# Who issues the down weights of the experts: ScalarE, behind its copy of the product, in place of SyncE

## The reference

```
u = x*(1+scale) + shift                       # (320, 1024)
s = sigmoid(u @ w_router)                     # 64 experts in 8 groups
idx, w = the best 8 experts of the best 4 groups, weights scaled to sum 2.5
routed = sum over the 8: w * ((silu(u @ w_gate[e]) * (u @ w_up[e])) @ w_down[e])
y = routed + swiglu(u, shared weights)
x = LayerNorm(alpha*x + (1+gate)*y)
```

## Time and profile before

| | |
|---|---|
| median of three runs | 2154.64 us |
| time of the profiled execution | 2159.98 us |
| its span, first to last instruction | 2158.5 us |
| TensorE busy in matmuls | 1803.2 us (84%) |
| VectorE, ScalarE, GpSimd busy | 705.2, 305.6, 364.2 us |
| experts of layer 0, first product to last | 397.1 to 951.4 us |
| experts of layer 1, first product to last | 1557.2 to 2098.9 us |

### The profile page before, as it was taken

The page is one execution under the profiler, slowest core; times in us unless marked ns, Lnnn a source line. Parts: engine busy times, 40 slices in busy tenths (PEclk is TensorE's granted clock), DMA queues, the critical chain, the costliest instruction groups (busy, mean ns, idle before and its releaser), DMA issues. The chain is left out here.

```text
span 2158.5 us, 32756 instructions
## 1 busy us (share of the span) xinstructions
PE 1803.2 (84%) x12297; PEld 1043.4 (48%) x12298; DVE 705.2 (33%) x1785; ACT 305.6 (14%) x639; POOL 364.2 (17%) x469
## 2 busy tenths in 40 slices
PE   6998977688888987775999998988488889987775
PEld 4555644344445543442556555544344455544442
DVE  1111237312233332216302444443611423331226
ACT  0221211000111110100122222221110111110010
POOL 3000100222222222210001012110022222222210
PEclk8999988799999999988798799997699999999997
DMA  9488965699999999959324389981699999999976
GB/s 348 147 314 307 366 231 234 259 424 416 387 383 403 418 411 393 408 229 333 105 70 162 103 275 284 294 279 66 270 402 422 415 399 404 422 408 407 403 290 219
DMA packets 133127, 675.12 MB, mean 313 GB/s; under 512 B 28432, under 2 KB 41360, under 8 KB 92709
## 3 DMA queue, kind: packets, MB, share of 16 engines
q1 hardware_dynamic: 84880, 570.20, 66.9%
q10 hardware_dynamic: 22180, 56.23, 7.7%
q0 software_dynamic: 25968, 47.32, 6.1%
HBM read 651.29 MB, written 47.99 MB: 324 GB/s over the span
## 5 line engine op out<-in xcount | busy, mean ns | idle before, releaser
L2292 PE MATMUL bank<-ring,work 128*64 128x256 f32 x4096 | 536.7, 421 | 143.3 <-DMA ring<-in_exp_w 140.0
L2292 PEld LDWEIGHTS bank<-ring,work 128*64 128x64 f32 x4096 | 340.5, 152 | 308.8 <-issue 130.2
L2020 PE MATMUL bank<-ring,uT 128*128 128x512 f32 (+1 forms) x896 | 256.7, 503 | 1.9 <-ACT work L1002 0.9
L2304 PE MATMUL bank<-ring,work 128*64 128x512 f32 x1032 | 249.9, 605 | 1.3 <-DVE work L1741 1.0
L788 POOL DMA_INDIRECT work<-u_d,work x128 | 130.6, 1020 | 640.5 <-DVE work L1707 334.8
L1707 DVE COPY work<-work 128x1 int32<-128x1 int32 (+1 forms) x128 | 19.3, 153 | 530.5 <-ACT work L1161 529.7
L2020 PEld LDWEIGHTS bank<-ring,uT 128*128 128x128 f32 (+1 forms) x896 | 119.4, 169 | 131.3 <-issue 115.7
L795 POOL DMA_INDIRECT pair_d<-work x128 | 132.6, 1036 | 267.6 <-DVE work L1711 250.1
L1161 ACT ACTIVATE work<-bank 128x128 f32<-128x128 f32 x128 | 35.5, 277 | 674.1 <-PE bank L2292 674.1
L1157 ACT COPY work<-bank 128x512 f32<-128x512 f32 x128 | 74.9, 585 | 292.7 <-PE bank L2304 292.7
L2284 PE MATMUL bank<-ident,work 128*128 128x128 f32 x516 | 97.5, 312 | 21.6 <-DMA work<-u_d,work 21.6
(11 more groups left out here) (357 smaller groups left out, 1721.6 us busy)
## 6 DMA issues: line engine op xcount, KB each, us to landing
ring<-in_exp_w SPq DMA_DIRECT2D x128, 2048.0 KB, 17.9
ring<-in_exp_w SPq DMA_DIRECT2D x128, 1024.0 KB, 13.0
ring<-in_ada_w SPq DMA_DIRECT2D x24, 2048.0 KB, 10.9
ring<-in_cache_k SPq DMA_DIRECT2D x128, 256.0 KB, 4.2
ring<-in_cache_v SPq DMA_DIRECT2D x128, 256.0 KB, 5.5
ring<-in_gla_w_in SPq DMA_DIRECT2D x6, 2048.0 KB, 17.2
ring<-in_kv_w_mod SPq DMA_DIRECT2D x4, 2048.0 KB, 11.4
work<-pair_d ACTq DMA_DIRECT2D x4, 2048.0 KB, 9.6
```

Source lines behind the costliest of these rows:

```text
L2020: ins = mm(out, uT[:, c, t0:t0 + r], ring_pair(unit)[:, c, cols], start=(c == 0), stop=(c == KT - 1), skip_group_check=(t == ST))
L2292: ins = mm(psum[s][64 * c:64 * c + 64, 0:2 * P].rearrange("p (a n) -> p a n", a=2), xT[:, s, j * P + 64 * half:j * P + 64 * half + 64], gu ...
L2304: ins = mm(psum[3 + s][64 * c:64 * c + 64, :], hT[:, s, 64 * f:64 * f + 64], w[:, f, c * 512:(c + 1) * 512], start=(f == 0), stop=(f == 1) ...
```

## The change

SyncE no longer waits for `y_full` and no longer issues the down weights for e from 3 on. ScalarE issues them instead, right behind the copy of the down product of e-1: the transfer of the down weights of e+2, which goes to the same slot. The down weights of the first three experts of each layer are still issued by SyncE.

```diff
                 def steady(e, s):
                     sp.wait_ge(h_full, e + (base - 2))
                     load_expert(l, e, s)
-                    sp.wait_ge(y_full, e + (base - 2))
-                    load_down(l, e, s)
...
+                def load_down(e, s):
+
+                    act.dma_start(ring[:, 3 * s + 2, :],
+                                  W["exp_w"][l, ds(e, 1)].rearrange("o p n -> p (o n)")[:, 2 * UNIT:3 * UNIT])\
+                       .then_inc(unit_full[3 * s + 2], 16)
+
-                def one(e, s, i, first=False):
+                def one(e, s, i, first=False, more=True):
                     act.wait_ge(h_full, e + (base + 1))
                     act.activation(sil[:, s, :], psum[s][:, 0:P], ACT.Silu).then_inc(sem("sil_ready"), 1)
                     if not first:
                         y_out(e - 1, (s + 2) % 3, stored_before(e - 1, (s + 2) % 3, i))
+                        if more:
+                            load_down(e + 2, (s + 2) % 3)
...
                 for e in range(60, 64):
-                    one(e, e % 3, 0)
+                    one(e, e % 3, 0, more=e + 2 < NE)
```

## The result

The changed kernel is slower by a third of a per cent: ratio 1.0035 to the kernel before, 95% interval 1.002 to 1.005 (20 runs of each; medians 2159.68 and 2153.42 us). On the median of the prediction that is 2154.64 x 1.0035 = 2162.2 us, +7.5 us. The forecast was 2154.3 us and no change that can be told; 0.22 was given to slower. The second rival, with half its stalls, had 2162 us too; what follows shows that its mechanism is at most a part of the loss, so that agreement is luck.

A forecast was written before the change was run, and what follows sets the result against it. The expert stages were taken as bound by DMA bytes, not by when transfers are issued. Terms -2.3 + 0 + 2.0 = -0.3 us gave 2154.3 us on the median, range 2145 to 2164.

The forecast's parts named there:

- The second rival: Expert stages, slower: down weights in q10 wait behind load_gate's rows; 2168 us, or 2162 with half the stalls; chance 0.18.
- A third busy queue: Gathers in q0 beside busy q10: they take 9.4 us, issued 13 us ahead at the least; 0, bounds 0 and +2.
- The signs that were named: Expert stages: earlier L620 issue, start hole gone, gate/up landing 20 us or more, down 8 to 10, in_exp_w wait near 140.
- Start of each layer's experts: At 410 to 412 and layer 1's start, earlier gate and up weights fill idle DMA engines: -2.3 us, bounds 0 and -2.8.
- Holes in the middle: Six 20 us stretches around the shared expert lack 9.8 us of DMA share; counted as 0, bounds 0 and -9.8.
- The argument from the lagging engines: In the middle holes the share bottoms at 0.27 and 0.25: engines finishing a transfer never pause, so earlier issue gains 0.
- the holes are real: Faster rival: each of the six middle holes is recovered too, -12.1 us, 2142.5 us, or 2147 with half; chance 0.27.
- Order of the bytes: Down weights share engines with gate and up weights, which land later at the layers' ends: +2.0 us, bounds 0 and +3.9.
- ScalarE's part: One DMA issue per expert on ScalarE, 0.33 to 0.45 us, hidden before a Silu that waits for TensorE: 0.
- Two streams at once: Expert stages: alternating between two queues costs no DMA rate; 0, bounds -3 and +3.
- Down weights behind the row loads: Slower rival: row loads in q10 delay down weights, TensorE waits 4 us at three places; 12 us if engines dry; chance 0.18.
- The rule that was cited: Issuing engines' queues end on the same 16 DMA engines, so the change can move order, not rate; no size.

The follow-up runs named there:

- late issue: Changed kernel with SyncE's old wait put back, gate and up weights of e issued only behind the down product of e-4: 1.0027 of the kernel before.
- the run with short gathers: Changed kernel with layer 1's gathers and scatters cut from 128 to 64 partitions: 0.9965; the kernel before with the same cut 0.9957, so 1.0008 between them.
- the run with rows of 8 KB: Changed kernel with gate and up weights in two transfers of 128 rows of 8 KB: 1.0031 of the kernel before.
- the one with even and odd halves: Changed kernel with gate and up weights in two transfers, of the 64 even and the 64 odd partitions: 1.0005 of the kernel before.
- the one-queue kernel: Kernel before with gate and up weights issued early and down weights after them, both by SyncE in q1: 0.9972 of the kernel before.

## Why the prediction was wrong

- **The step that failed** is "A third busy queue", put at 0 with bounds of 0 and +2 us. It took the 9.4 us of rows 10, where q10 carried rows of 4 KB for a while, as what gathers take beside a second queue. The gathers went to 15.9 us, TensorE's wait for them from 21.6 to 155.4 us, and with the second queue of weights the time is 0.27% (late issue) to 0.63% (early issue) longer than without it. The working for the rivals had the tool at hand, in "on an engine q10 must pass 8 + 28 + 8 rows, each beside one of 16 KB": turns by row. It was never applied to q0, whose gather and scatter have 8 rows each per expert and engine, in 8 packets and 2 small ones. Before, these 10 met 18 packets in one other queue; after, they meet 9 and 9 in two queues, and every queue gets one turn in a round. What is shown is that the second queue of weights costs the time. That it does so through the gathers is argued: for it are the waits and the run with short gathers; against it as the whole cause are the run with rows of 8 KB (no such waits, 1.0031), the one with even and odd halves (128.8 us of them, 1.0005), and the stage of layer 1 that shrank with the stall as well. How the loss divides between the gathers, the down weights behind the row loads and the clock that fell behind a long wait (0.66 from 1985 to 2005) stays open.
- **The signs that were named**: issue to landing was to rise for gate and up weights to 20 us or more, and to fall for down weights to some 8 to 10. It fell to 14.3 and rose from 13.0 to 14.0; and the wait for gate and up weights, which was to stay near 140 us, went. The forecast took the weights as what TensorE waits for in either kernel.
- **Start of each layer's experts**, -2.3 us: the hole closed as worked out, 0.18 and 0.44 became 0.96 and 0.99 in layer 0. What that is worth was not measured by itself.
- **Holes in the middle**, 0: wrong in sign. They grew, by 6.0 us in the 80 us of layer 1 shown above. The argument from the lagging engines was not put to a test by itself. In the one-queue kernel the same two stretches have shares of 1.00 and 0.98, for 0.96 and 0.97, so earlier issue does seem to shrink them, and its gain of 0.28%, 6 us (2 to 10 by the interval), is more than the 2.3 us of the starts. For the early issue alone the remainder of some -4 us would belong here, by subtraction; if so, the rival "the holes are real" had this half right.
- **Order of the bytes**, +2.0 us at the ends: the mechanism is not what came. TensorE's last expert of layer 1 starts at 2092.91 for 2090.82, 2.1 us later, which looks like the term, but 8.2 us later when measured from the layer's first product. All weights are in before it starts, and it is the last gathers and the lower clock behind them that hold TensorE up.
- **ScalarE's part**, 0: nothing speaks against it; two issues per expert in the run with all weights on ScalarE still gave 0.9965.
- **Two streams at once**, 0: in a full stretch the rate is as before (from 1591 to 1631 the changed kernel has 424 GB/s at a share of 1.01), so no term there.
- **Down weights behind the row loads**: the rival's mechanism is real, with one landing worked out at 40.4 us behind the last row load and found at 39.2. Its price was put at 12 us with the engines running dry; 3 us of free engines stand behind the one in layer 1. What the stalls cost in all was not isolated; that layer 1's stage lost 6 us of its excess where they were gone says that it may be more than 3.
- **The rule that was cited** from the Trainium skill ("DMA: Bandwidth & Descriptors", section "Issuing engines are not separate DMA queues"), that spreading DMAs over issuing engines saves only issue time, holds for the rate and says nothing of what decided: the share of each queue. And the rule of the Trainium skill on arbitration ("DMA: Bandwidth & Descriptors", section "Queues, rings and completion order") has a whole packet per turn, some 9 to 17 descriptors. The trace agrees with the turn of one packet, but its packets hold one row of weights or two rows of a gather, so the eight rows of a transfer do not stay together.

## What to carry to other kernels

In this kernel's traces the DMA engines served the queues by turns of one packet, whatever its size (16 KB, 8 KB or 4 KB). Moving a part of the weights to a queue of its own leaves the other queues more turns to wait for, so count, for each queue, packets per engine and step before and after, the small indirect transfers above all: they have few bytes and many packets (10% of the engines' time here, and as many packets as each queue of weights). If transfers are to be issued earlier, keep them in one queue in the order of their use; here that turned 1.0035 into 0.9972 from SyncE and 0.9965 from ScalarE, the fastest of the versions that compute the same result, though the two can't be told apart.

## What the hardware showed beyond what was expected

- Two transfers of 64 neighbouring partitions in place of one of 128 run at 228 GB/s with all engines busy, against 415 for even and odd partitions: 1.404 of the time of the whole program.
- With rows of 8 KB in place of 16 KB, the DMA engines move 402 to 408 GB/s at a share of 1.00, in place of 409 to 413.
- Rows of an indirect transfer that fall beyond the bound keep their packets: with 18.69 MB cut to 9.63 in layer 1, q0 has 25968 packets over the whole profile as before, and the gathers landed in 14.3 us in place of 16.0.
- The engines go round the queues packet by packet: in the changed kernel q1, q10 and q0 have 8327, 8803 and 9144 packets from 1580 to 2080, of 16 KB, 8 KB and 4 KB at the most, and mostly follow each other in this order.
